# Differential attention steps: negated scores, lambda as a second scalar, GpSimd work in four pieces, the short transpose first, one projection ahead of a head's scores

## The reference, cut to what matters

```python
def attend(qb):
    s = jnp.einsum('bqhcd,bkhcd->bhcqk', qb, k).astype(jnp.float32) * scale
    p = jax.nn.softmax(s, axis=-1)
    a = p[:, :, 0] - lam_f * p[:, :, 1]
    o = jnp.einsum('bhqk,bkhd->bqhd', a, vf)
    return o.astype(v.dtype)
...
o = rms_norm_2(o, subln_gain[li]) * (1.0 - lambda_init)
y = jnp.concatenate([f_out, a_out], axis=-1) * jax.nn.silu(gate)
h_res = h_res + y @ w_out[li]
```

## Time and profile before

| | |
|---|---|
| median of 3 runs | 3711.67 us (3711.29 to 3716.3) |
| profiled execution, device time | 3714.64 us |
| its span in the profile | 3712.8 us |
| mean granted TensorE clock | 0.964 |
| busy: PE, DVE, ACT, POOL | 92%, 57%, 42%, 37% of the span |
| chain that ended last, by engine | PE 69%, DVE 11%, issue 8%, ACT 5% |

### The profile page before, as it was taken

One profiled execution on the slowest core, in us unless ns is written; L12 is line 12 of the kernel. 1 busy time (PEld: TensorE's weight loads), 2 busy tenths in 40 slices (PEclk: granted clock), 3 DMA queues, 4 the chain that ended last, 5 costly groups with the idle time before them and its releaser, 6 DMA issues.

```text
span 3712.8 us, 59979 instructions
## 1 busy us (share of the span) xinstructions
PE 3408.3 (92%) x18080; PEld 2760.3 (74%) x18080; DVE 2127.6 (57%) x5374; ACT 1563.8 (42%) x3221; POOL 1379.3 (37%) x1578
## 2 busy tenths in 40 slices
PE   8999998998999999999999989889888998898878
PEld 6878886665778888876666779777766798677756
DVE  5666665665256666657663441476663423676653
ACT  6444443443245544434442431355452312555532
POOL 6555544333516555543335312122231222222231
PEclk9999999999999999999999999999998999899989
DMA  4111112111221111121112221211121511111124
GB/s 147 33 35 34 34 40 55 38 41 46 85 89 40 32 33 34 34 57 43 38 35 86 86 74 52 55 32 27 38 75 49 164 46 56 32 38 37 45 65 145
DMA packets 217950, 206.47 MB, mean 56 GB/s; under 512 B 17948, under 2 KB 185260, under 8 KB 216668
## 3 DMA queue, kind: packets, MB, share of 16 engines
q1 hardware_dynamic: 197536, 137.80, 13.3%
q0 software_dynamic: 12208, 47.03, 3.7%
q10 hardware_dynamic: 7920, 18.19, 1.5%
HBM read 148.04 MB, written 37.01 MB: 50 GB/s over the span
## 4 chain that ended last, share of the span: by engine, by line
PE 69%; DVE 11%; issue 8%; ACT 5%; DMA 3%; POOL 1%; DVEq 1%; SPq 1%; ACTq 0%; POOLq 0%
PE banks L1006 22%; PE banks L1290 8%; PE banks L1175 5%; PE banks L1227 5%; PE banks L1308 4%; PE banks L1199 4%; PE banks L1372 3%; PE banks L1121 2%; PE banks L1131 2%; PE banks L1252 2%; PE banks L1143 1%; PE banks L1350 1%; PE banks L1044 1%; DVE BB L2069 1%; PE banks L1363 1%
## 5 line engine op out<-in xcount | busy, mean ns | idle before, releaser
L1006 PE MATMUL banks<-H,whi 128*128 128x512 f32 x3200 | 1047.7, 409 | 20.9 <-POOL wlo L670 19.1
L1006 PEld LDWEIGHTS banks<-H,whi 128*128 128x128 f32 x3200 | 573.9, 189 | 199.7 <-issue 80.6
L1006 PE MATMUL banks<-H,wlo 128*128 128x512 f32 x1600 | 632.6, 395 | 0.0
L669 POOL CAST whi<-raw 128x1024 fp32r<-128x1024 f32 x150 | 164.2, 1094 | 1096.4 <-PE banks L1006 433.0
L1290 PE MATMUL banks<-H,whi 128*128 128x346 f32 (+1 forms) x1536 | 384.4, 333 | 10.1 <-DVEq L423 8.0
L670 POOL TENSOR_TENSOR wlo<-raw,whi 128x1024 fp32r<-128x1024 f32 x150 | 363.6, 2424 | 12.1
L1006 PEld LDWEIGHTS banks<-H,wlo 128*128 128x128 f32 x1600 | 302.2, 189 | 69.5
L2380 DVE TENSOR_SCALAR_CACHE_REDUCE SP<-banks 128x346 f32<-128x346 f32 (+3 forms) x432 | 201.4, 513 | 248.3 <-PE banks L1351 246.8
L1290 PEld LDWEIGHTS banks<-H,whi 128*128 128x128 f32 x1536 | 275.6, 195 | 20.4 <-issue 15.0
L1648 ACT ACTIVATE SM<-SM,stt 128x256 f32<-128x256 f32 (+1 forms) x256 | 124.8, 488 | 333.4 <-DVE stt L2226 333.4
L1290 PE MATMUL banks<-H,wlo 128*128 128x346 f32 (+1 forms) x768 | 252.2, 328 | 0.0
(11 more groups left out here) (313 smaller groups left out, 7492.5 us busy)
## 6 DMA issues: line engine op xcount, KB each, us to landing
raw<-in_w_in SPq DMA_DIRECT2D x148, 512.0 KB, 3.9
raw<-in_w_out SPq DMA_DIRECT2D x64, 256.0 KB, 2.6
XT<-x_resident POOLq DMA_DIRECT2D x18, 512.0 KB, 4.1
x_resident<-XT POOLq DMA_DIRECT2D x18, 512.0 KB, 2.9
raw<-in_w_out SPq DMA_DIRECT2D x18, 512.0 KB, 5.2
RQ<-QR SPq DMA_DIRECT2D x112, 64.0 KB, 2.0
XB<-x_resident POOLq DMA_DIRECT2D x14, 512.0 KB, 4.6
SR<-cat_resident SPq DMA_DIRECT2D x16, 448.0 KB, 4.2
```

The lines of the kernel that those rows point to most:

```text
L669: link(nc.gpsimd.tensor_copy(hi, src))
L1006: last = nc.tensor.matmul(bank(half if bk is None else bk), w[:, slot, k, :], H[:, part, a:a + 512], start=k == 0 and n == 0, stop=k == DT ...
```

## The change

It touches five things. The evacuation multiplies the scores by -1 and accumulates the minimum, so the reduction gives the negated maximum at once, the exponential takes scale -1, and the instruction that negated goes. `combine` scales component 1 with two scalars in one instruction (its reciprocal sum and minus lambda) and then adds component 0 times its scalar, so the small product goes. GpSimd's subtractions in `split_tile` and for the output weights, and all three instructions of `roped2`, are issued as four of a quarter's width (the casts stay whole; the splits of other stages too). `transposes2` turns the 16-key tile first. And at block 0 of heads 1 to 3 TensorE issues the items of `first` ahead of its waits and of the scores.

```diff
-         "act_B": 17, "dve_B": 193, "pool_B": 38, "phases_B": 1}
+         "act_B": 17, "dve_B": 121, "pool_B": 38, "phases_B": 1}
...
+            def split(e, slot, hi, lo, src, parts=1):
                 link(nc.gpsimd.tensor_copy(hi, src))
-                nc.gpsimd.tensor_tensor(lo, src, hi.bitcast(F32), ALU.subtract).then_inc(g("w_split"), 1)
+                n = src.shape[-1] // parts
+                for a in range(0, n * parts, n):
+                    last = nc.gpsimd.tensor_tensor(lo[:, a:a + n], src[:, a:a + n], hi[:, a:a + n].bitcast(F32), ALU.subtract)
+                last.then_inc(g("w_split"), 1)
...
-                    split_in(wp + GROUPS + n // 2, n % 2, used)
+                    split_in(wp + GROUPS + n // 2, n % 2, used, 4)
...
-                    nc.gpsimd.tensor_tensor(QN[:, m, :], QN[:, m, :], rope2[:, 0, :], ALU.mult)
-                    link(nc.gpsimd.tensor_tensor(RT[:, :], RT[:, :], rope2[:, 1, :], ALU.mult))
-                    nc.gpsimd.tensor_tensor(QN[:, m, :], QN[:, m, :], RT[:, :], ALU.add).then_inc(g("rp_ready"), 1)
+                    parts = [slice(a, a + T2 // 4) for a in range(0, T2, T2 // 4)]
+                    for t in parts:
+                        nc.gpsimd.tensor_tensor(QN[:, m, t], QN[:, m, t], rope2[:, 0, t], ALU.mult)
+                    for t in parts:
+                        last = nc.gpsimd.tensor_tensor(RT[:, t], RT[:, t], rope2[:, 1, t], ALU.mult)
+                    link(last)
+                    for t in parts:
+                        last = nc.gpsimd.tensor_tensor(QN[:, m, t], QN[:, m, t], RT[:, t], ALU.add)
+                    last.then_inc(g("rp_ready"), 1)
...
-                    for n, tiles in enumerate(((0, 1, 2, 3), (4, 5, 6, 7), (8,))):
+                    for n, tiles in enumerate(((8,), (0, 1, 2, 3), (4, 5, 6, 7))):
...
+                    if i == 0 and 0 < h < HEADS2:
+                        for it in first:
+                            item(*it)
+                        first = []
...
-                            last = nc.scalar.activation(SP[0:nq, t % 2, c, :], SP[0:nq, t % 2, c, :], ACT.Exp, bias=st[:, 8 + c:9 + c], accum_out=st[:, 10 + c:11 + c])
+                            last = nc.scalar.activation(SP[0:nq, t % 2, c, :], SP[0:nq, t % 2, c, :], ACT.Exp, scale=-1.0, bias=st[:, 8 + c:9 + c], accum_out=st[:, 10 + c:11 + c])
...
-                    V.tensor_scalar(SP[0:nq, t % 2, c, a:a + n], psum[2 + k % 3][0:nq, 0:n], 1.0, None, ALU.mult, ALU.max,
+                    V.tensor_scalar(SP[0:nq, t % 2, c, a:a + n], psum[2 + k % 3][0:nq, 0:n], -1.0, None, ALU.mult, ALU.min,
...
-                    link(V.tensor_tensor(st[:, 14:15], st[:, 13:14], nlam[0:nq, :], ALU.mult))
-                    link(V.tensor_scalar(SP[0:nq, t % 2, 0, :], SP[0:nq, t % 2, 0, :], st[:, 12:13], None, ALU.mult))
-                    V.scalar_tensor_tensor(SP[0:nq, t % 2, 0, :], SP[0:nq, t % 2, 1, :], st[:, 14:15], SP[0:nq, t % 2, 0, :], ALU.mult, ALU.add).then_inc(g("pr_ready"), 1)
+                    link(V.tensor_scalar(SP[0:nq, t % 2, 1, :], SP[0:nq, t % 2, 1, :], st[:, 13:14], nlam[0:nq, :], ALU.mult, ALU.mult))
+                    V.scalar_tensor_tensor(SP[0:nq, t % 2, 0, :], SP[0:nq, t % 2, 0, :], st[:, 12:13], SP[0:nq, t % 2, 1, :], ALU.mult, ALU.add).then_inc(g("pr_ready"), 1)
...
-                        link(V.tensor_reduce(st[:, 6:8], st[:, 0:6].rearrange("p (c j) -> p c j", c=2), AX_X, ALU.max))
-                        V.tensor_scalar(st[:, 8:10], st[:, 6:8], -1.0, None, ALU.mult).then_inc(g("m_ready"), 1)
+                        V.tensor_reduce(st[:, 8:10], st[:, 0:6].rearrange("p (c j) -> p c j", c=2), AX_X, ALU.min).then_inc(g("m_ready"), 1)
```

More of the change, by code:

```diff
@@ L663, in _ @@
                     pool.wait_ge(g(name), 1)
-            def split(e, slot, hi, lo, src):
+            def split(e, slot, hi, lo, src, parts=1):
                 pool.wait_ge(g(f"w_in{slot}"), e * 16 + 16)
@@ L669, in split, with split_in @@
                 link(nc.gpsimd.tensor_copy(hi, src))
-                nc.gpsimd.tensor_tensor(lo, src, hi.bitcast(F32), ALU.subtract).then_inc(g("w_split"), 1)
-            def split_in(e, slot, used):
+                n = src.shape[-1] // parts
+                for a in range(0, n * parts, n):
+                    last = nc.gpsimd.tensor_tensor(lo[:, a:a + n], src[:, a:a + n], hi[:, a:a + n].bitcast(F32), ALU.subtract)
+                last.then_inc(g("w_split"), 1)
+            def split_in(e, slot, used, parts=1):
                 if used is not None:
                     pool.wait_ge(g("proj_ready"), used)
-                split(e, slot, whi[:, slot, :, :].rearrange("p t e -> p (t e)"), wlo[:, slot, :, :].rearrange("p t e -> p (t e)"), raw[:, slot, :])
+                split(e, slot, whi[:, slot, :, :].rearrange("p t e -> p (t e)"), wlo[:, slot, :, :].rearrange("p t e -> p (t e)"), raw[:, slot, :], parts)
             for e in range(2):
@@ L925, in _ @@
                     if n % 4 < 2:
-                        split(wp + GROUPS + 2 * HEADS2 + n // 4, n % 4, WH2[:, n, :], WL2[:, n, :], raw[:, n % 4, :])
+                        split(wp + GROUPS + 2 * HEADS2 + n // 4, n % 4, WH2[:, n, :], WL2[:, n, :], raw[:, n % 4, :], 4)
                     else:
-                        split(L * 2 + n // 4, n % 4, WH2[:, n, :], WL2[:, n, :], raw2[:, n % 4 - 2, 0:D])
+                        split(L * 2 + n // 4, n % 4, WH2[:, n, :], WL2[:, n, :], raw2[:, n % 4 - 2, 0:D], 4)
                 for n in range(EARLY2):
@@ L1903, in _ @@
                             ps = psum[5 + (3 * (t - 1) + n) % 2]
-                            if n < 2:
-                                last = nc.scalar.copy(A2T[:, 4 * n:4 * n + 4, q0:q0 + nq], ps.rearrange("p (k q) -> p k q", q=P)[:, :, 0:nq])
+                            if n:
+                                last = nc.scalar.copy(A2T[:, 4 * n - 4:4 * n, q0:q0 + nq], ps.rearrange("p (k q) -> p k q", q=P)[:, :, 0:nq])
                             else:
```

## The result

| | runs | median us | lowest to highest |
|---|---|---|---|
| before | 4 | 3711.48 | 3707.71 to 3716.30 |
| after | 4 | 3681.57 | 3678.75 to 3686.93 |

A forecast was written before the change was run, and what follows sets the result against it. The prediction took TensorE, busy 92% of the span, as the bound, so only its waits or slower running counted. Terms summed to 19.8 us a layer, 39.6 in all, giving 3672 us from a median of 3711.7; range 3650 to 3694.

The forecast's parts named there:

- Short transposes first: Transposes in the steps: the 16-key tile's earlier copy removes TensorE's waits for a free bank; 5.7 us a layer, bounds 0 to 6.6.
- Small instructions removed: VectorE's `combine` and negation: 0.3 us at each of five waits, 0.7 at one late step; 2.2 us a layer.
- The scaling with two scalars: In `combine`: takes 0.76 us, as with one scalar; upper bound 1.30, costing 6.5 us a layer.
- rival C: Scaling with two scalars runs at 1.30 us, so 13 us of the gain go: 3685 us; chance 0.05.
- GpSimd's pieces: Subtractions cut in four take 2.59 us instead of 2.42, 0.17 more; the extra stays hidden, also in head 3.
- Turns, instruction by instruction: VectorE and GpSimd alternate on SBUF operands, so successive VectorE instructions each wait for a piece, nearly one whole instruction's cost.
- rival A: VectorE needn't take turns: a piece holds up one instruction and the rest pass; 9 us a layer more, 3654; chance 0.13.
- Before head 0: VectorE's chain waits less for GpSimd at two places, 0.35 and 1.4 us; 1.7 us a layer, bounds 0 to 4.
- The projection ahead: Starts of heads 1 to 3: projection matmuls cover TensorE's wait for queries; 6.4 us a layer, bounds 2.2 to 10.
- Rival B: Latency moves: ScalarE delays the short copy, or a new wait behind scores takes all but 2.2 us; 3692; chance 0.12.
- Head 3: Steps 3 to 6, where GpSimd splits output weights: shorter waits give 2.2, 1.5, 0.7 and 0.4, in all 4.8 us.
- Clock: New waits of 2 us at the heads' starts can make TensorE's clock fall again: -1.0 us a layer.

The follow-up runs named there:

- u_scores_first: The changed kernel with the projection behind the head's first scores again, as before the change; 0.9904 of the kernel before.
- a_pair_late: The changed kernel with ScalarE's logarithm and exponential for the inverse root moved behind the three copies of the transposes; 0.9943 of the kernel before.

## Why the prediction was right, and where it was not

3681.6 us lies inside 3650 to 3694, and the direction held. The size came out of errors of both signs, so that the range was met is in part luck. Per layer: 19.8 us forecast; 14.3 measured in the steps and 3.0 before head 0, 17.3. Of the forecast, 20.8 were waits and -1.0 the clock. Of the measured, the waits gave 11.0 (8.0 in the steps, 3.0 before head 0), about half; the clock gave 2.8 and TensorE's work 3.5, which no term of the sum had. What each undoing costs below has its own share of the clock in it.

- *Short transposes first, 5.7.* Undoing it costs 8.2 a layer in the steps, but only 1.7 of that is waits, the thing that was priced. 4.7 are the matmul that starts sooner when a full transpose is ahead of it, which the sum left out, and 1.9 the clock. The first group's copy was as early as forecast in most steps, and the waits of 0.24 us are gone; where ScalarE is late, in six steps of a layer, TensorE now waits 1.2 to 1.6 us behind the short tile.
- *Small instructions removed, 2.2.* Undoing them costs 6.5 a layer: 3.2 of open time, near the forecast, 2.3 of the clock, and the rest work. But they did not come where forecast. "0.3 each at five waits" did not reach TensorE: in the steps with sums ScalarE ended last. The sum took VectorE's time as TensorE's without asking who comes next. The gain came at the starts of heads 1 and 2, in head 3 and in two steps of head 0.
- *The scaling with two scalars at 0.76.* It measures 0.807 to 1.821, median 0.821: 0.06 more, far from the 1.30 of rival C.

```profile
L2402 DVE TENSOR_SCALAR SP<-SP,st,nlam x72: 807/821/1821, 2408.0 to 3579.5; 128x1040 f32<-128x1040 f32 x64, 16x1040 f32<-16x1040 f32 x8
```

- *GpSimd's pieces, 0.17 more a split.* Too cheap. Where VectorE does little but empty PSUM banks beside them, four take 2.81 us (second fence below) against 2.35 to 2.42 whole: 0.4 to 0.45 more. The 0.17 came from another stage's 256-wide instruction. The kernel before has a 512-wide one of 1.285 us (first fence), and two of these are 0.15 more than a 1024-wide one; three cuts at that rate are 0.44, as measured. Beside VectorE it is more: the output weights' pieces took 0.925 us each, 3.70 a split where one whole took 2.63, 8.6 us over eight, and the last ended 37.7 us after the first began instead of 34.7. The products y never waited for it, as forecast; but it was not hidden, since the low parts and `combine` ahead of them met it (under head 3).

```profile
L784 POOL TENSOR_TENSOR RQ<-RQ,ropet 128x512 f32<-128x512 f32 x32 | 41.1, 1285 | 0.0
```

```profile
2417.94 2.81 POOL L672 TENSOR_TENSOR wlo<-raw,whi 128x256 fp32r<-128x256 f32 x4
...
L672 POOL TENSOR_TENSOR H<-raw,H 128x256 fp32r<-128x256 f32 x32 | 28.7, 925 | 0.6
```

- *Turns, instruction by instruction.* Right, and rival A wrong. Before head 0 each of VectorE's instructions that ran bare in 1.24 us takes 0.42 more beside the pieces, and the pieces stretch to 6.70 us:

```profile
2373.89 1.96 DVE L2357 SCALAR_TENSOR_TENSOR SR<-SR 128x1040 f32<-128x1040 f32 x1
2374.84 6.70 POOL L672 TENSOR_TENSOR wlo<-raw,whi 128x256 fp32r<-128x256 f32 x4
2375.89 1.66 DVE L2358 TENSOR_TENSOR SR<-SR 128x1040 f32<-128x1040 f32 x1
```

- *Before head 0, 1.7.* Measured 3.0, inside its bounds of 0 and 4.
- *The projection ahead, 6.4.* The wrong step, and the largest. "A new wait of some 2 us stands ahead of the transposes": in head 1 there are two, 2.50 and 1.61 us, since the six scores pairs need VectorE to empty three banks between them. The three heads' waits for queries, 9.5 us in u_scores_first's first layer, are gone; the waits that came in their place left 1.4 us a layer of gain in open time, and the clock took 6.3. The move costs 5.4 us a layer. Rival B's second half had the new wait take the gain, all but 2.2; it did not have the move cost anything. That its 3680 is close to the time measured is chance, since other terms were off the other way.
- *Head 3, 4.8.* From the end of head 2's last transposes, head 3 gave 1.3 us in the first layer (125.7 to 124.4) and 3.6 in the second (125.6 to 122.0); the clock's share in it rose by 1.8 us in the first and fell by 1.5 in the second. "The wait of 4.57 comes by way of ScalarE: 0.7 gained" was wrong in sign: it grew to 6.76. TensorE and VectorE come earlier, the split of the output weights takes longer, and so `low_mixed` and `combine` now meet it, which before ran free of GpSimd.
- *Clock, -1.0.* Wrong in sign and size. The steps' half-clock time fell by 15.5 us a layer, but 9.9 of that was time in which TensorE was idle anyway; the other 5.6, in which work takes double, are worth 2.8. It was priced at one place only, and every wait removed or split up elsewhere has its share: of the four undoings, those of the pieces and of the move are mostly clock.

The move and head 3 were oversized by far, the first two and the pieces undersized. In waits alone the forecast missed half; the clock and the order of the transposes, which it did not have, made up most of that.

## What to carry to other kernels

A wait removed from TensorE is not yet time won: ask which engine comes last next, and add up TensorE's busy time as well as its waits, since the same matmuls can take 10 us more where more of them fall into a half-clock stretch. Take half of the busy time at half clock off first: what is left should not move, and where it does, as with the short transpose, there is something else to find. Moving work ahead of a wait only helps if what it covered before is covered by something else. Where a wait cannot be removed and falls just ahead of dense work, cheap useless matmuls in it can keep the clock up; here they did when they filled all of a 9.7 us wait but 1.4, and filling half of it bought little.

## What the runs showed of the hardware

- TensorE's work at 1.2 GHz takes twice its time, and that explains the busy time: 762.7 to 789.3 us over nine runs with the short tile first and no transposes added, 730.7 to 735.4 with half of the busy time at half clock taken off.
- The half-clock stretches belong to the program more than to the run: repeated, the first layer's steps took 441.2 and 441.1 us, with 55.2 and 55.1 us at half clock, the second layer's 439.4 and 441.3 with 49.2 and 55.4. Against that, an edit that left open time within 0.6 us moved 34 us of half-clock time into both layers (a_pair_late). A wait of 9.7 us before head 0 filled for 5.4 moved the fall 3.4 and 6.8 us later; filled but for 1.4 it removed it.
- Short waits of some 4 us in sum can be followed by a fall or not: head 1 had 4.1 us (2.50 and 1.61) with one, and 3.75 (2.94 and 0.81) without. What decides between these two was not tried.
- Behind the transpose of the 16-key tile the next matmul starts 0.12 to 0.19 us later, behind one of 128 columns 0.03.
- VectorE and GpSimd take turns on SBUF operands by whole instructions and in both directions; cut GpSimd's, and the delay of VectorE's 1.24 us instructions falls from 2.08 us to 0.42, while GpSimd's four pieces grow from 2.81 us to as much as 6.70.
